# Six projection steps of the second block: three narrow matmuls become one wide and one narrow, and the two halves of the sum meet on VectorE

## The reference, cut to what matters

```
h = rms_norm(x, g_attn_pre[l]) * (1.0 + scale_a[:, None]) + shift_a[:, None]
proj = h @ w_in[l]
parts = [proj[..., offsets[i]:offsets[i + 1]] for i in range(len(PROJ_SIZES))]
d_q, d_k, d_v, s_q, s_k, s_v, i_q, i_k, i_w = parts
...
d_q, d_k and s_q (1024 columns each): partial_rope, then attention
i_q, i_k, i_w: scores, top-k selection and masks of the sparse attention
```

## Time and profile before

| | |
|---|---|
| median of 3 runs | 2504.49 us (2504.17 to 2506.11) |
| the profiled execution's own time | 2503.54 us |
| span of its profile | 2501.8 us |
| mean granted TensorE clock | 0.996 |
| PE / PEld / DVE / ACT busy | 99% / 84% / 71% / 49% |
| the six narrow steps, first matmul to the first of the value step | 1435.45 to 1591.31 us, 155.86 us |

### The profile page before, as it was taken

The page is one execution under the profiler, slowest core; times in us unless marked ns, Lnnn a source line. Parts: engine busy times, 40 slices in busy tenths (PEclk is TensorE's granted clock), DMA queues, the critical chain, the costliest instruction groups (busy, mean ns, idle before and its releaser), DMA issues.

```text
span 2501.8 us, 33253 instructions
## 1 busy us (share of the span) xinstructions
PE 2474.9 (99%) x13327; PEld 2108.4 (84%) x13327; DVE 1787.2 (71%) x2453; ACT 1229.9 (49%) x1802; POOL 0.5 (0%) x5
## 2 busy tenths in 40 slices
PE   9999999999999999999999999999999999999998
PEld 8888877888888888888887899877788888888887
DVE  6557767677788788788788768777766556665555
ACT  6456456444554444443444444565544444443553
POOL 0000000000000000000000000000000000000000
PEclk9999999999999999999999999999999999999999
DMA  8555455888778879879788555555677667667554
GB/s 275 196 187 179 160 173 172 311 313 274 255 266 302 283 255 328 280 264 327 261 280 295 181 177 160 161 173 201 211 235 235 216 213 236 219 197 207 187 184 134
DMA packets 325446, 573.25 MB, mean 229 GB/s; under 512 B 28690, under 2 KB 124204, under 8 KB 324652
## 3 DMA queue, kind: packets, MB, share of 16 engines
q1 hardware_dynamic: 278300, 449.45, 54.5%
q10 hardware_dynamic: 46992, 121.68, 13.9%
HBM read 561.36 MB, written 8.60 MB: 228 GB/s over the span
## 4 chain that ended last, share of the span: by engine, by line
PE 94%; DVE 3%; ACT 2%; issue 1%; DMA 0%; ACTq 0%; SPq 0%; DVEq 0%
PE ps L501 28%; PE ps L546 14%; PE ps L548 14%; PE ps L547 14%; PE ps L505 14%; PE ps L1064 2%; PE ps L1065 2%; PE ps L1066 2%; DVE wl L1865 1%; ACT wh L1153 1%; DVE ts L2011 1%; DMA raw<-w_in 0%; PE ps L993 0%; PE ps L949 0%; PE ps L811 0%
## 5 line engine op out<-in xcount | busy, mean ns | idle before, releaser
L1865 DVE TENSOR_TENSOR wl<-raw,wh 128x1024 fp32r<-128x1024 f32 x856 | 1040.2, 1223 | 675.6 <-ACT wh L1153 673.3
L1153 ACT ACTIVATE wh<-raw 128x1024 fp32r<-128x1024 f32 x856 | 898.8, 1058 | 1057.9 <-PE ps L548 498.4
L501 PE MATMUL ps<-hs,wh 128*128 128x512 f32 x3144 | 992.0, 397 | 2.1 <-DVE hs L1959 0.9
L505 PEld LDWEIGHTS ps<-hs,wl 128*128 128x128 f32 x3144 | 591.2, 188 | 140.7
L505 PE MATMUL ps<-hs,wl 128*128 128x256 f32 x3144 | 619.0, 278 | 0.0
L501 PEld LDWEIGHTS ps<-hs,wh 128*128 128x128 f32 x3144 | 480.3, 189 | 4.8 <-issue 2.0
L546 PE MATMUL ps<-wh,ff 128*128 128x512 f32 x864 | 336.1, 389 | 0.0
L547 PE MATMUL ps<-wl,ff 128*128 128x512 f32 x864 | 336.1, 389 | 0.0
L548 PE MATMUL ps<-wh,ff 128*128 128x512 f32 x864 | 336.1, 389 | 0.0
L546 PE MATMUL ps<-wh,hs 128*128 128x512 f32 x640 | 256.8, 401 | 0.3 <-DVE wl L1865 0.3
L548 PE MATMUL ps<-wh,hs 128*128 128x512 f32 x640 | 250.0, 391 | 0.0
(11 more groups left out here) (304 smaller groups left out, 1764.5 us busy)
## 6 DMA issues: line engine op xcount, KB each, us to landing
raw<-w_in SPq DMA_DIRECT2D x111, 1024.0 KB
raw<-w_down SPq DMA_DIRECT2D x108, 1024.0 KB
raw<-w_up SPq DMA_DIRECT2D x64, 1024.0 KB
ada_w<-w_ada ACTq DMA_DIRECT2D x96, 512.0 KB, 5.5
ada_more<-w_ada ACTq DMA_DIRECT2D x96, 512.0 KB, 6.1
raw<-w_gate SPq DMA_DIRECT2D x88, 512.0 KB
raw<-w_up SPq DMA_DIRECT2D x88, 512.0 KB
raw<-w_out SPq DMA_DIRECT2D x16, 1024.0 KB
```

The costliest lines, as they stand in the source:

```text
L501: nc.tensor.matmul(ps[0:m, b, :], wh[:, slot, w0:w0 + m], rhs(n, k), start=k == 0, stop=False)
L505: mm = nc.tensor.matmul(ps[0:m, b, 0:T], wl[:, slot, w0:w0 + m], rhs(n, k)[:, 0:T], start=False, stop=k == 4 * panels - 1)
L1153: nc.scalar.activation(wh[:, h % WH_SLOTS, :], raw[:, slot, HALF * q:HALF * (q + 1)], ACT.Copy).then_inc(wh_ready, 1)
L1865: nc.vector.tensor_tensor(wl[:, h % WH_SLOTS, :], raw[:, slot, HALF * q:HALF * (q + 1)], wh[:, h % WH_SLOTS, :], ALU.subtract).then_inc(wl ...
```

## The change

The three matmuls per k become the wide pair, in the order wide, wide, low, low. ACT's `narrow_out` copies the right halves to `te` instead of the whole tile to `z`, counting a new semaphore `right_copied`; it now also waits until the previous step's tile has been added (`proj_copied`), since `te` is reused. A new `narrow_out` on DVE adds left half and `te` into `z` and counts `proj_copied`. It stands in DVE's loop at n = 31, 39, 47, 55, 63 and 71, behind `heads_of_second(n - 1)` and ahead of `feed(n + 4)`. DMAs and SP's queue are as before.

```diff
@@ narrow_step, on PE
-                            sums = ps[:, n, 0:T]
-                            nc.tensor.matmul(sums, wh[:, slot, w0:w0 + m], hs[:, k, 0:T], start=k == 0, stop=False)
-                            nc.tensor.matmul(sums, wl[:, slot, w0:w0 + m], hs[:, k, 0:T], start=False, stop=False)
-                            mm = nc.tensor.matmul(sums, wh[:, slot, w0:w0 + m], hs[:, k, T:2 * T], start=False,
+                            nc.tensor.matmul(ps[:, n, :], wh[:, slot, w0:w0 + m], hs[:, k, :], start=k == 0, stop=False)
+                        for kk in range(2):
+                            k = 2 * h + kk
+                            w0 = 512 * kk + c0
+                            mm = nc.tensor.matmul(ps[:, n, 0:T], wl[:, slot, w0:w0 + m], hs[:, k, 0:T], start=False,
                                                   stop=k == ND - 1)
@@ narrow_out, on ACT
-                    nc.scalar.activation(z[:, narrow_tile(i, n), :], ps[:, n, 0:T], ACT.Copy
-                                         ).then_inc(sem("proj_copied"), 1)
+                    if i:
+                        act.wait_ge(sem("proj_copied"), 4 * i - 3 + n)
+                    nc.scalar.activation(te[:, n, :], ps[:, n, T:2 * T], ACT.Copy).then_inc(sem("right_copied"), 1)
@@ on DVE
+            def narrow_out(i):
+
+                for n in range(4):
+                    dve.wait_ge(sem("right_copied"), 4 * i + n + 1)
+                    nc.vector.tensor_tensor(z[:, narrow_tile(i, n), :], ps[:, n, 0:T], te[:, n, :], ALU.add
+                                            ).then_inc(sem("proj_copied"), 1)
+
             for n in range(24, 104):
+                if n < 72 and n % 8 == 7:
+                    narrow_out(n // 8 - 3)
                 feed(2 * L7.panel + n + 4, 0)
                 heads_of_second(n)
```

## The result

The changed kernel takes 2515.49 us in the median (2514.29 to 2516.51, 4 runs) against 2504.33 us; the ratio is 1.0043, 95% interval 1.0031 to 1.0055. It is slower by 11.2 us, where 7.8 were forecast: the direction and the range held (2506.5 to 2516.5, near its top), the size was short by 3.4 us. The profiled execution took 2514.96 us with a span of 2513.2.

What follows compares the result with a forecast made beforehand. PE's pace, or what makes PE wait, was taken to bound the kernel. A gain of 4.4 us against waits of 10.8 and one clock fall of 1.4 gave +7.8: 2512.3 us, 0.3% slower, range 2506.5 to 2516.5.

Steps and rivals of the forecast that it cites:

- stop at border 0 to 1: Between narrow steps 0 and 1, PE waits for DVE to finish rope until 1461.02 and add: 1.64 us.
- 3 to 4: Between narrow steps 3 and 4, PE waits for DVE, without pause through rope and top-k: 3.74 us.
- into the value step: After the last narrow step, ACT's second copy is late, so the second add and PE are late: 0.7 us.
- What bounds, and the pace: In the six narrow steps PE's pace sets the time; 0.349 us for 0.360 over 384 pieces gains 4.4 us.
- The copies and the load on DVE: In the narrow steps, 24 ACT copies stay 0.381 us each; DVE's 24 adds, 10 us of work, cost nothing as throughput.
- The new wait: At six borders PE waits for DVE's adds, queued behind feed and attention work: 10.8 us in all.
- The clock: Behind PE's long stop at border 3 the granted clock falls to 0.50 once: +1.4 us.
- the rival with three falls: The clock falls behind each long stop, at borders 1, 2 and 3: 2515.1 us, chance 0.17.
- the forecast's own case: Waits of 9 to 12 us at the borders with one clock fall, at most two: 2512.3 us, chance 0.62.
- VectorE was in time: Rival: DVE adds when te is ready, no border costs anything, whole 4.4 us gained: 2500.1 us, chance 0.09.
- Shorter waits: Rival: borders 0 to 2 at half price, 3 as computed, no clock fall: 2507.9 us, chance 0.12.
- The rule on queues: VectorE and ScalarE work strictly in order, so a ready add can't pass a rope or top-k instruction; no size given.

Runs made afterwards that it cites:

- the last experiment: From the kernel in which ACT frees both halves of the bank, VectorE's adds moved behind heads_of_second(n) of half 7: 2507.12 us against 2504.88 for the kernel before.
- Three traces: Traces of the changed kernel (2515.49 us), of narrow matmuls with copy and VectorE maximum at the adds' places (2516.39), and of the changed kernel rerun (2515.05).

## Why the prediction was right in direction and short in size

| term | predicted us | measured us |
|---|---|---|
| gain of the wide form | -4.4 | -4.4 (alone, in whole runs; -4.2 in the six steps) |
| stop at border 0 to 1 | 1.64 | 1.72 |
| 1 to 2 | 2.22 | 2.20 |
| 2 to 3 | 2.22 | 2.21 |
| 3 to 4 | 3.74 | 3.63 |
| 4 to 5 | 0.3 | 0.3 |
| into the value step | 0.7 | 0.5 |
| clock falls | 1 x 1.4 | 3 x 1.6 |
| sum | +7.8 | +11.1 (six steps, by the timeline) |

- **What bounds, and the pace.** Right, and shown: alone, the wide form gives the 4.4 us that the two rows of pace gave.
- **The copies and the load on DVE.** Right, and shown by the kernel in which ACT frees the bank: 24 adds more on DVE and 24 longer copies on ACT cost 1.0 us in the six steps.
- **The new wait.** Right at five borders to 0.1 us and at the last to 0.2, and shown twice: the wait alone, without the wide form, makes the same stops, and moved ahead of one half's attention work they shrink to 4.1 us in all. What made the sum come out is that each stop was counted on DVE's queue from its last idle moment, not from a mean load.
- **The clock.** This is the step that was mis-sized: "so I count one such fall: +1.4". The mechanism was right, its count was not. The stops of 2.1 us drew the clock down too, in the profiled execution both of them; with 1.6 for 1.4 us a fall, the term is 4.8 us for 1.4, which is the 3.4 us that the prediction lacked. So what came is the rival with three falls, 2515.1 us, and not the forecast's own case of one fall, at most two; the time lies in the range because the range reached up to that rival, and the six steps, 166.96 us, are beyond the 162 to 164 that were expected. That rival had a chance of 0.17 with the argument that the only case in the trace had a second stop close behind the first; one stop was enough. The size of 1.4 us was read too low as well: in that case the clock was at 0.50 already ahead of PE's first wide matmul at 1369.98, while PE stood idle, so a part of the fall cost nothing.

```profile
1369.60:1370.00 0.40, 0.02 (x1) 0.05 (x1) 0.40 (x2) 0.00 (x0) 0.00 (x0) 0.50 1.05 410
```

- **The other rivals.** VectorE was in time nowhere but at border 4, as forecast. Shorter waits did not come: DVE's chains started from PE's own halves.
- **The rule on queues.** The strict order that the Trainium skill ("TensorE: Matmul & The Clock Gate", Engine queue depths) gives for VectorE and ScalarE held in every row looked at. In the last experiment a place one half further back in that order cost 5.6 us: the adds behind a top-k piece on VectorE, the bank copy behind late exponentials on ScalarE.

What stays open: what decides whether a stop of 2.1 us is followed by a fall. Three traces with such stops show it behind both, behind the third only, and behind the second only; the stops of 1.5 to 1.9 us drew none (the first one in each of these traces, and the one left with the adds ahead), and those of 3.3 to 3.6 us drew one each time.

## What to carry to other kernels

A job moved to another engine is priced by where that engine's queue stands when the result is wanted, not by its load: DVE worked 76% of the stretch before, and yet PE stood 1.7 to 3.6 us for it at four borders, because its lateness had until then been covered by four prepared halves and a bank to be freed has no such cover. Free the bank with the engine that is in time, and let the busy engine finish from SBUF; that turned +11.2 us into -3.3. Then look who else waits for the result: a wait ahead of a DMA in a queue holds up everything behind it.

## What the runs showed of the hardware that was not expected

- Stops of PE of 2.1 us can be enough for the granted clock to go from 1.00 to 0.50: it fell behind four of the six in the three traces, and a fall cost 1.6 us. Filling four stops with 36 unread matmuls took 4.9 us off the six steps.
- The clock can fall when PE is already running again. In the changed kernel's trace the third stop ended at 1518.89, and PE's groups slowed from 1520.39 on; behind the second stop the first group was slow from its start at 1489.42.
